# The feed-forward output product by one level of Strassen's recursion

## The reference

```
def conv_gated_ffn(h, w_in, conv_w, conv_b, w_out):
    s = h.shape[1]
    a = h @ w_in
    gate, up = a[..., :FFN_DIM], a[..., FFN_DIM:]
    gpad = jnp.pad(gate, ((0, 0), (CONV_WIDTH - 1, 0), (0, 0)))
    conv = conv_b + sum(gpad[:, tap:tap + s] * conv_w[tap] for tap in range(CONV_WIDTH))
    return (jax.nn.silu(conv) * up) @ w_out
```

## Time and profile before

| | us |
|---|---|
| median of 3 runs | 1498.79 (1498.66 to 1498.87) |
| profiled execution, its own time | 1498.81 |
| its span, first to last instruction | 1496.9 |
| PE busy | 1483.0 |
| DVE busy | 847.7 |
| ACT busy | 675.6 |
| POOL busy | 796.9 |
| granted TensorE clock, mean share of full | 0.998 |

### The profile page before, as it was taken

How to read it: one execution, slowest core, us unless ns; L and a number is a source line. 1 busy time by engine, 2 the same in 40 slices (tenths; PEclk the granted TensorE clock), 3 DMA queues, 4 the chain that set the end, 5 groups by cost and what they waited for, 6 DMA issues and landing times.

```text
span 1496.9 us, 19989 instructions
## 1 busy us (share of the span) xinstructions
PE 1483.0 (99%) x6808; PEld 1235.4 (83%) x6808; DVE 847.7 (57%) x1294; ACT 675.6 (45%) x1019; POOL 796.9 (53%) x980
## 2 busy tenths in 40 slices
PE   9999999999999999999999999999999999999997
PEld 6888888888888888888888888888888888888886
DVE  7999997455555411169875655646655555511145
ACT  6887886433333322246573543635633333322243
POOL 5343344666666755457345253551666666755453
PEclk9999999999999999999999999999999999999999
DMA  4121111323222322243132322321232222332221
GB/s 179 57 71 55 43 56 59 111 99 98 98 98 98 126 99 97 86 163 105 56 141 99 109 90 90 134 99 43 85 113 91 96 92 98 120 111 97 93 79 63
DMA packets 42838, 142.14 MB, mean 95 GB/s; under 512 B 4256, under 2 KB 10528, under 8 KB 42784
## 3 DMA queue, kind: packets, MB, share of 16 engines
q1 hardware_dynamic: 41248, 138.82, 27.2%
q10 hardware_dynamic: 1536, 2.61, 0.5%
HBM read 139.32 MB, written 2.10 MB: 94 GB/s over the span
## 4 chain that ended last, share of the span: by engine, by line
PE 96%; DVE 2%; ACT 1%; DMA 1%; issue 0%; POOL 0%; SPq 0%; POOLq 0%; DVEq 0%; ACTq 0%
PE bank L606 27%; PE bank L610 26%; PE bank L609 26%; PE bank L884 3%; PE bank L889 3%; PE bank L888 3%; PE bank L684 2%; PE bank L664 1%; PE bank L665 1%; PE bank L695 1%; PE bank L694 1%; DMA x<-in_xT 1%; PE bank L1037 0%; DVE sumsq L1126 0%; PE bank L667 0%
## 5 line engine op out<-in xcount | busy, mean ns | idle before, releaser
L552 POOL TENSOR_TENSOR wl<-raw,wh 128x256 fp32r<-128x256 f32 x752 | 617.4, 853 | 471.1 <-ACT wh L1712 471.1
L606 PE MATMUL bank<-xh,wh 128*128 128x512 f32 (+1 forms) x1160 | 451.6, 389 | 1.2 <-POOL wl L552 0.8
L610 PE MATMUL bank<-xh,wl 128*128 128x512 f32 (+1 forms) x1160 | 450.2, 388 | 0.0
L609 PE MATMUL bank<-xl,wh 128*128 128x512 f32 (+1 forms) x1160 | 449.9, 388 | 0.0
L1712 ACT ACTIVATE wh<-raw 128x1024 fp32r<-128x1024 f32 (+1 forms) x212 | 234.9, 1108 | 475.3 <-PE bank L606 387.6
L606 PEld LDWEIGHTS bank<-xh,wh 128*128 128x128 f32 x1160 | 217.9, 188 | 46.8 <-DVE xl L1132 1.7
L610 PEld LDWEIGHTS bank<-xh,wl 128*128 128x128 f32 x1160 | 217.9, 188 | 44.9
L609 PEld LDWEIGHTS bank<-xl,wh 128*128 128x128 f32 x1160 | 218.0, 188 | 43.8
L568 POOL TENSOR_TENSOR wl<-raw,wh 128x256 fp32r<-128x256 f32 x160 | 127.3, 826 | 190.6 <-ACT wh L1712 190.6
L1152 DVE TENSOR_TENSOR x<-x,bank 128x512 f32<-128x512 f32 x56 | 38.5, 687 | 251.1 <-PE bank L610 251.1
L610 PE MATMUL bank<-yh,wl 128*128 128x512 f32 x352 | 137.0, 389 | 0.0
(11 more groups left out here) (224 smaller groups left out, 2325.2 us busy)
## 6 DMA issues: line engine op xcount, KB each, us to landing
raw<-in_w SPq DMA_DIRECT2D x180, 512.0 KB, 3.2
raw<-in_w SPq DMA_DIRECT2D x32, 704.0 KB, 4.0
rc<-in_w SPq DMA_DIRECT2D x16, 512.0 KB, 4.1
w_end<-in_w SPq DMA_DIRECT2D x8, 512.0 KB, 4.2
rb<-in_w SPq DMA_DIRECT2D x8, 512.0 KB, 6.1
x<-in_xT SPq DMA_DIRECT2D x4, 512.0 KB, 7.2
pin<-in_pT ACTq DMA_DIRECT2D x2, 512.0 KB, 3.2
rotary<-in_consts ACTq DMA_DIRECT2D x1, 512.0 KB, 3.5
```

Source lines behind the costliest of these rows:

```text
L552: last = nc.gpsimd.tensor_tensor(wl[:, slot, cols], part[:, cols], wh[:, slot, cols].bitcast(F32), ALU.subtract)
L606: first = mm(out, ah_, bh_, start=start, stop=False, skip_group_check=True)
L609: mm(out, ah_, bl_, start=False, stop=False, skip_group_check=True)
L610: return mm(out, al_, bh_, start=False, stop=stop, skip_group_check=True)
```

## The change

Both layers' output products are done by one level of Strassen's recursion, in the form with seven products. The weight is cut in four: output chunks 4 to 7 (A11, A12) and 0 to 3 (A21, A22), even chunks of y (A11, A21) and odd ones (A12, A22). The tokens are cut in two halves, so y is Y11, Y12 (even chunks, early and late tokens) and Y21, Y22 (odd chunks). Four weight sums are formed: S1 = A21 + A22, S3 = A11 + A21, S2 = S3 + A22, S4 = S2 + A12. Each of the seven products has four pieces (one for each output chunk of a half), 28 pieces in the order of `PIECES`, and a piece is 11 blocks of three matmuls of 256 columns.

For each piece ScalarE makes the high part, GpSimd the low part of two blocks and VectorE that of the other nine (`POOL_BLOCKS = 2`); VectorE makes the sixteen weight sums of 11x128 columns, takes the 28 results out of PSUM into x, and makes the low parts of the right-hand operands (five splits of 11x256 columns, `right_lows`, and the difference `t4`, done beside the pieces; two more splits and three sums or differences of y's quarters stand in the loop of the feed-forward input). 22 loads of 704 KB take the place of 16. The squares of x go to SBUF rather than PSUM. The load of `pin` and its splits come later in the stage. On VectorE the low part of piece 0 stands behind the loop over y.

```diff
+PIECES = ([("A11", m) for m in range(K2)]
+          + [(kind, m) for m in range(K2) for kind in ("S1", "S3")]
+          + [("S2", 0), ("S2", 1), ("A22", 0), ("S2", 2), ("A22", 1), ("S2", 3), ("A22", 2), ("A22", 3)]
+          + [("S4", 0), ("S4", 1), ("S4", 2), ("A12", 0), ("S4", 3), ("A12", 1), ("A12", 2), ("A12", 3)])
...
+POOL_BLOCKS = 2
...
+LOADS = ([("A11", 0, "s0"), ("A11", 1, "r0"), ("A11", 2, "r1"), ("A21", 0, "r0"), ("A22", 0, "r1"),
+          ("A11", 3, "s3"), ("A11", 1, "s1"), ("A11", 2, "s2"), ("A21", 1, "r0"), ("A22", 1, "r3"),
+          ("A22 again", 2, "r2"), ("A21", 2, "r0"), ("A22", 2, "r1"), ("A21", 3, "r0"), ("A22", 3, "r3")]
+         + [("A22 again", 0, "r0"), ("A22 again", 1, "r1"), ("A22 again", 3, "r3")]
+         + [("A12", m, f"r{m}") for m in range(K2)])
...
+        REGION = {"r0": raw[:, 0:FH * P].rearrange("p (a c) -> p a c", c=P),
+                  "r1": raw[:, RAW_COLS // 2:RAW_COLS // 2 + FH * P].rearrange("p (a c) -> p a c", c=P),
+                  "r2": in_y[:, :, 0, 0:P], "r3": in_y[:, :, 0, P:HALF],
+                  **{f"s{m}": s_[:].rearrange("p (a c) -> p a c", c=P) for m, s_ in enumerate(S_BUFFER)}}
...
+                for what, m, into in LOADS:
+                    if (what, m) == ("A11", 0):
+                        sp_eng.wait_ge(w_low, end - 2)
+                    elif what == "A11" and into[0] == "r":
+                        sp_eng.wait_ge(w_low, end - 2 + m)
+                    elif (what, m) == ("A21", 0):
+                        piece_low(PIECE["A11", 1])
+                    elif (what, m) == ("A22", 0):
+                        piece_low(PIECE["A11", 2])
+                    elif into == "s3":
+                        sp_eng.wait_ge(f_begun, f_count(layer, 0))
+                    elif into[0] == "s":
+                        sp_eng.wait_ge(y_full, FC * (layer + 1))
...
+            def piece_lows(layer):
+                for q in range(N_PIECES):
+                    held = [blocked(part[:, piece_slot(layer, q), :]) for part in (wh, wl)]
+                    pool.wait_ge(f_high, f_count(layer, q))
+                    for b in range(0, POOL_BLOCKS, LOW_BLOCKS):
+                        part = slice(b, b + LOW_BLOCKS)
+                        last = nc.gpsimd.tensor_tensor(held[1][:, part, :], piece_source(q)[:, part, :],
+                                                       held[0][:, part, :].bitcast(F32), ALU.subtract)
+                    last.then_inc(f_low_p, 1)
...
+                for q, (kind, m) in enumerate(PIECES):
+                    out = bank[m if kind in ("S1", "S4") else K2 + m][:, 0:HALF]
+                    opens = kind in ("A11", "S1", "A12")
+                    pe.wait_ge(f_low_p, f_count(layer, q))
+                    pe.wait_ge(f_low_v, f_count(layer, q))
...
+                        before = {"S3": "A11", "S2": "S3", "A22": "S2", "S4": "S1", "A12": "A22"}[kind]
+                        pe.wait_ge(f_freed, f_count(layer, PIECE[before, m]))
+                        pe.wait_ge(right_low, 5 * layer + ready[kind])
...
+                        last = three(out, *blk(piece_slot(layer, q), k), high[:, k, :], low_[:, k, :], opens and k == 0,
+                                     k == FH - 1, begins=k == 0, begun=f_begun)
+                    last.then_inc(f_prod, 1)
...
+                def low_part(q):
+                    part = slice(POOL_BLOCKS, FH)
+                    held = [blocked(part_[:, piece_slot(layer, q), :])[:, part, :] for part_ in (wh, wl)]
+                    dve.wait_ge(f_high, f_count(layer, q))
+                    low(held[1], piece_source(q)[:, part, :], held[0], f_low_v)
...
+                def right_lows(j, out, full, high, sign):
+                    dve.wait_ge(right_high, 5 * layer + j)
+                    if sign > 0:
+                        low(out[:], full, high[:], right_low)
+                    else:
+                        vec.scalar_tensor_tensor(out[:], full, -1.0, high[:].bitcast(F32), ALU.mult, ALU.subtract)\
+                            .then_inc(right_low, 1)
+                def t4():
+                    dve.wait_ge(right_low, 5 * layer + 2)
+                    vec.tensor_tensor(Y12, Y21, Y12, ALU.subtract).then_inc(t4_full, 1)
+                def take(q):
+                    kind, m = PIECES[q]
+                    dve.wait_ge(f_prod, f_count(layer, q))
+                    if q:
+                        dve.wait_ge(f_freed, f_count(layer, q - 1))
+                    part = bank[m if kind in ("S1", "S4") else K2 + m][:, early]
+                    first, second = x[:, K2 + m, :], x[:, m, :]
+                    if kind == "A11":
+                        both = first.rearrange("p (a t) -> p a t", a=2)
+                        last = vec.tensor_tensor(both, both, part.unsqueeze(1).to_broadcast([P, 2, HALF]), ALU.add)
+                    elif kind == "S2":
+                        vec.tensor_tensor(first[:, late], first[:, late], part, ALU.add)
+                        last = vec.tensor_tensor(second[:, late], second[:, late], part, ALU.subtract)
+                    else:
+                        x_, cols, sign = {"S1": (second, late, ALU.subtract), "S3": (first, late, ALU.subtract),
+                                          "A22": (second, early, ALU.subtract), "S4": (first, late, ALU.add),
+                                          "A12": (first, early, ALU.add)}[kind]
+                        last = vec.tensor_tensor(x_[:, cols], x_[:, cols], part, sign)
+                    last.then_inc(f_freed, 1)
...
+                beside = {
+                    0: lambda: sum1(0),
+                    1: lambda: (right_lows(1, zl, Y11, zh, 1), sum3(0)),
+                    3: lambda: (sum1(1), sum3(1)),
+                    5: lambda: (sum1(2), sum3(2)),
+                    6: lambda: (right_lows(2, xa_l, Y12, xa_h, -1), t4()),
+                    7: lambda: (sum1(3), sum3(3)),
+                    9: lambda: (sum2(0), sum2(1)),
+                    11: lambda: sum2(2),
+                    12: lambda: right_lows(3, ya_l, Y12, ya_h, -1),
+                    13: lambda: sum2(3),
+                    15: lambda: norm_open(norm),
+                    16: lambda: (sum4(0), x_lows(0)),
+                    17: lambda: (squares(0), sum4(1)),
+                    18: lambda: (right_lows(4, xa_l, Y22, xa_h, 1), x_lows(1)),
+                    19: lambda: (sum4(2), squares(1)),
+                    20: lambda: (sum4(3), x_lows(2)),
+                    21: lambda: (right_lows(5, ya_l, Y21, ya_h, 1), squares(2)),
+                    22: lambda: (x_lows(3), squares(3)),
+                    24: p_lows,
+                    25: lambda: (x_lows(4), squares(4)),
+                    27: lambda: (x_lows(5), squares(5)),
+                    28: lambda: (x_lows(6), squares(6)),
+                }
+                for q in range(2):
+                    low_part(q)
+                for j in range(N_PIECES + 1):
+                    if j:
+                        take(j - 1)
+                    if j + 2 < N_PIECES:
+                        low_part(j + 2)
+                    if j in beside:
+                        beside[j]()
...
+                        vec.tensor_tensor(one(y, f), cv, up[:], ALU.mult).then_inc(y_full, 1)
+                        if u == 0:
+                            dve.wait_ge(y_full, at + 1)
+                            vec.tensor_tensor(one(y, f)[:, late], one(y, f)[:, early], one(y, f)[:, late], ALU.subtract)\
+                                .then_inc(t1_full, 1)
+                            dve.wait_ge(y11_high, FH * layer + i + 1)
+                            low(one(xa_l, i), one(y, f)[:, early], one(xa_h, i), y11_low)
+                        else:
+                            dve.wait_ge(y_full, at + 1)
+                            vec.tensor_tensor(one(y, f - 1)[:, late], one(y, f)[:, late], one(y, f - 1)[:, late], ALU.add)\
+                                .then_inc(t2_full, 1)
+                            dve.wait_ge(t2_full, FH * layer + i + 1)
+                            vec.tensor_tensor(one(y, f - 1)[:, early], one(y, f - 1)[:, late], one(y, f - 1)[:, early],
+                                              ALU.subtract).then_inc(t3_full, 1)
+                out_stage(layer, norm + 1)
...
+            def piece_high(layer, q):
+                kind, m = PIECES[q]
+                if q < RING - 1:
+                    act.wait_ge(w_begun, N_PL[layer] - RING + q + 2)
+                else:
+                    act.wait_ge(f_begun, f_count(layer, q - RING + 1))
+                if kind[0] == "S":
+                    made = {"S1": f_sum1, "S3": f_sum3, "S2": f_sum2, "S4": f_sum4}[kind]
+                    act.wait_ge(made, layer * K2 + m + 1)
...
+                def right_highs(j, out, full, sign):
+                    if j == 1:
+                        act.wait_ge(t3_full, FH * (layer + 1))
+                        act.wait_ge(f_begun, f_count(layer, 0))
```

(38 more changed lines are left out.)

274 lines of the change are left out of this document (201 added, 73 removed).

## The result

The changed kernel takes 1528.29 us (median; 1526.77 to 1530.14), the kernel before it 1498.74: a ratio of 1.0198, 95% interval 1.018 to 1.0215. Forecast were 1510.0 and a range of 1490 to 1524. The sign was right, the size was not: 29.5 us more instead of 11.3. The profiled execution took 1526.77 us, the shortest of the four.

A forecast was written before the change was run, and what follows sets the result against it. TensorE, busy 1483.0 of 1496.9 us, was taken as the bound. A layer: -8.8 + 4.2 + 6 + 3 = +4.4; two +8.8, clock +2.5, so 1498.8 + 11.3 = 1510 us, range 1490 to 1524.

The forecast's parts named there:

- TensorE's own row: Output stage: 924 matmuls of 256 columns, 0.120 us each, replace 528 at 0.2267; 8.8 us less a layer.
- the opening: Before the first output matmul, TensorE waits for VectorE's nine low blocks of piece 0: 4.2 us in each layer.
- up to piece 9: VectorE's queue makes low part 9 late, so TensorE loses 6 us a layer; bounds 3 and 8.
- pieces 10 to 23: VectorE's 56.3 us with GpSimd against TensorE's 55.4 leaves no cushion: 3 us a layer, bounds 0 and 7.
- clock after that: Clock may fall to half after four waits of over 4 us in two layers: 2.5 us for all four.
- Waits for loads and for ScalarE: VectorE before low part 9: 4.2 us for A22 0's load, 3.3 for later loads and ScalarE's copies.
- VectorE's instructions: VectorE's low parts, takes, sums, `right_lows` and `t4` before low part 9: 32.7 us; GpSimd adds up to 3.2.
- The signs that I named for "wrong": Gap ahead of piece 9 under 2 us, or low parts and sums taking clearly more or less than priced.
- VectorE keeps up: Rival: in the output stage only the opening's wait is left, 9.2 us less in all, 1490; chance 0.24.
- GpSimd stops VectorE for its whole 0.82 us: Rival: in the output stage each piece costs VectorE 0.46 us more, 13 us a layer, 1536; chance 0.07.

The follow-up runs named there:

- e3: Changed kernel with A11 3 loaded ahead of A21 0 and the A11 1 and 2 loads for the sums held until piece 2 begins: 1523.83 us.
- e1: Changed kernel with spare 256-column matmuls filling TensorE's waits ahead of pieces 0, 4, 6 and 9: 1527.76 us.
- e9: `right_lows` 2 and 5 each a step earlier, against a kernel with GpSimd opening, `t4` later, `right_lows` 1 earlier and loads reordered: 1508.26 us.
- e11: e9 with GpSimd in pieces 0 to 2 only, plus A22 3 loaded before A21 3, `right_highs` 5 earlier and `x_lows` 2 later: 1491.66 us.
- e6: Changed kernel without GpSimd in the stage, VectorE making all eleven low blocks: 1523.45 us.

## Why the prediction was wrong in size

Layer 0, term by term, as forecast and as the profile after has it:

| term | forecast | measured |
|---|---|---|
| TensorE's own row | -8.8 | -8.8 (matmuls 0.120 apart at full clock) |
| the opening | +4.2 | +4.2 (4.05 + 0.16) |
| up to piece 9 | +6, bounds 3 and 8 | +14.0: 10.1 in three waits, 3.9 of slow clock |
| pieces 10 to 23 | +3 | +2.5 |
| clock after that | +1.25 | +1.5 |
| sum | +5.6 | +13.4, against 13.8 by the stage's ends |

**The step that failed** is the queue up to piece 9. I let low part 9 be made 44.3 us after TensorE's last input tile; it was made at 570.4, 54.0 us after it. The 9.7 us are two terms of that sum:
- *Waits for loads and for ScalarE*: I had 4.2 and 3.3, 7.5 in all; the profile has 6.49, 0.84, 4.06, 2.32 and 0.44, 14.2. I priced each load at 4.0 us, from a stage where its median landing was 4.0, and argued that 138 GB/s on average leave room. At the first sum five loads were under way, and A22 0 took 6.3 to land: 2.3 more than I had. For the two loads after it I had about 1 us each, as if SP issued them when their own gate opened. They stood behind loads that wait for VectorE's sums, and cost 4.06 and 2.32. So both the landing time and the order of SP's queue were wrong in the sum; e3 takes 4.5 us off by spreading the first loads.
- *VectorE's instructions*: 32.7 forecast, some 35.8 measured; 2.2 of the difference are GpSimd's turns (0.55 at `zl`, 0.53 at the sum after it, 0.43 at `t4`, the rest at low parts). I had worked out up to 3.2 and let some of it count in the place of the waits. These 2.2 came on top. (The price of 0.36 for each of GpSimd's instructions was a misreading too: I had spread 0.55 over 1.5 of them, and a full turn costs 0.53 to 0.55. Not each of them cost a full turn: the 28 of a layer lengthened VectorE's instructions by some 8 us.)

Then I took 6 where my sum gave 4.5 to 7.7, and an upper bound of 8 that held no term for late loads.

**The clock** fell as I had it, after the waits ahead of pieces 0 and 9 in both layers, for 14 to 25 of a piece's 33 matmuls; what that costs I had wrong, since I added it on top. e1 shows how it enters: up to piece 9 a slow TensorE costs nothing, because VectorE decides when that piece starts. The 3.9 us of slow clock there are in the place of waits. Even the 1.5 us after piece 9 are a term of this profile's account rather than a saving to be had: at full clock piece 14 starts no earlier in layer 0, and 0.7 us earlier in layer 1. A fall after the wait ahead of piece 23 is paid in full, 1.5 us, where an execution has one (e1, e3 and e9 do, the changed kernel's profiled one does not). The Trainium skill (TensorE: Matmul & The Clock Gate, "Why this matters for your kernels") advises against idle gaps between bursts; in this case's trace the gaps themselves were the matter: spare matmuls in four of them bought 0.5 us in the median, less than the spread of the executions (1526.3 to 1529.2), and the clock fell after others.

**Right** were the saving of TensorE, the opening, the place of the longest later wait (piece 9, with `t4` and `right_lows` 2 ahead of its low part), and that pieces 10 to 23 have no cushion. The signs that I named for "wrong" did not show, or only in part: the gap at piece 9 is 4.4 us, and the low parts take 1.34 to 1.73, but five of the sixteen sums take 2.15 for 1.62. They were too few; I named none for the waits ahead of pieces 4 and 6 (2.4 and 2.9 us), and it is there that the loads showed.

**The rivals.** "VectorE keeps up" did not come about here, but it is what e11 makes of the same method: opening on GpSimd, later waits of 4.1 and 5.5 us in the two layers, and 7.1 us gained. The gain that the change could have is thus there; its order of work hid it. "GpSimd stops VectorE for its whole 0.82 us" gave 1536 and was nearer to the median than my forecast, but for another reason: by e6 all of GpSimd's share is worth 4.8 us. Of the mechanism I had thought too little. The Trainium skill (SBUF — State Buffer, "SBUF: two separate sides") has the two engines exclude each other for whole instructions, and I held against it, since 1.76 is less than 1.21 and 0.82. The turns above show the exclusion, and 1.76 is 1.21 and 0.55. For the length the measurement decides: GpSimd's instruction keeps VectorE out for 0.55 us of its 0.82, not for all of it, and that is what I had wrong.

## What to carry to other kernels

A transfer's price is read where as many are under way as will be after the change, and every wait in a DMA queue is followed to the loads behind it. A stage whose average leaves an engine 10% idle has no room if that engine is in order and waits early: sum the queue up to each hand-over, with its waits, and give those their own upper bound. When such a stage loses, look first at who does the work at its opening and at what each instruction waits for and lets go (e9 moved one instruction ahead of what it waits for and lost 2.7 us a layer); the same arithmetic ran 36.6 us faster here with another order and another owner.

## What the runs showed of the hardware

- VectorE (two SBUF inputs) and GpSimd take turns by whole instructions: a GpSimd difference of 128x256 adds 0.53 to 0.55 us to a VectorE instruction (1.62 to 2.15, 3.08 to 3.63), and itself takes up to 3.65 us beside one of 2816 columns, ending 0.59 us after it.
- A 704 KB load lands 4.1 us after its issue (median into `raw`), 7.6 to 10.2 as the third to fifth of five issued within 3 us; into `y`, where the program puts each block in pieces of 128 columns apart, 6.0 (whether that is the reason was not tried).
- After waits of TensorE of 4.05, 2.90, 4.36 and 4.48 us its clock was at the lower level for a while, and not after those of 2.39, 2.73, 2.58 and 1.99. In e1, where spare matmuls filled the longer waits, it was so after waits of 1.98, 2.10 and 1.99, so the length of the wait alone does not decide it. At that level matmuls of 256 columns start 0.213 us apart, 1.78 times 0.120, so even these small ones feel the clock almost in full.
